# The odd layer's short convolution, one pair of tiles later

## The reference, cut to what matters

```
qkv, z, a, bt = split_cols(h @ w_in, ODD_SPLITS)
qkv = jax.nn.silu(causal_dwconv(qkv, conv_w))     # 4 taps per channel, DN_CONV_K = 4
q, k, v = split_cols(qkv, ...)                    # 1024 channels each, 8 heads of 128
```

## Time and profile before

| what | value |
|---|---|
| median of 3 runs | 2412.43 us |
| the profiled execution | 2412.22 us |
| its span (first to last instruction) | 2410.5 us |
| PE busy | 1926.5 us (80%) |
| DVE busy | 966.3 us (40%) |
| ACT busy | 710.7 us (29%) |
| DMA | mean 252 GB/s |

### The profile page before, as it was taken

How to read it: one execution, slowest core, us unless ns; L and a number is a source line. 1 busy time by engine, 2 the same in 40 slices (tenths; PEclk the granted TensorE clock), 3 DMA queues, 4 the chain that set the end, 5 groups by cost and what they waited for, 6 DMA issues and landing times.

```text
span 2410.5 us, 30262 instructions
## 1 busy us (share of the span) xinstructions
PE 1926.5 (80%) x13238; PEld 1377.4 (57%) x13238; DVE 966.3 (40%) x1730; ACT 710.7 (29%) x1152; POOL 4.1 (0%) x11
## 2 busy tenths in 40 slices
PE   7689998879798999769868888978867765665656
PEld 6589997769678999447644332333255532232323
DVE  6866655666656665354462010101064510100101
ACT  5355444453434444334432000000034410000000
POOL 0000000000000000000000000000000000000000
PEclk9899999799999999989989999999988888888788
DMA  6234454321276445841134999999932379999997
GB/s 246 96 140 162 140 193 181 118 96 71 74 265 229 171 169 199 345 177 74 36 140 188 428 428 427 428 427 428 428 126 105 140 302 428 427 428 427 427 427 325
DMA packets 44787, 606.53 MB, mean 252 GB/s; under 512 B 5104, under 2 KB 5232, under 8 KB 6768
## 3 DMA queue, kind: packets, MB, share of 16 engines
q1 hardware_dynamic: 43488, 597.61, 61.2%
q0 software_dynamic: 880, 4.98, 0.6%
q10 hardware_dynamic: 288, 2.02, 0.2%
HBM read 603.54 MB, written 1.05 MB: 251 GB/s over the span
## 4 chain that ended last, share of the span: by engine, by line
PE 50%; DMA 27%; DVE 14%; ACT 6%; issue 2%; SPq 0%; DVEq 0%; ACTq 0%
PE ps L85 48%; DMA m_last_slot<-moe_down 15%; DMA m_more<-moe_up 9%; DVE m_WL L94 2%; PE ps L88 2%; ACT m_WH L91 1%; ACT m_mix_sc L91 1%; DVE m_od_low L100 1%; DMA m_ring<-ada 1%; DVE m_misc L103 1%; DVE m_wk L94 1%; DVE m_ev L94 1%; ACT m_od_low L91 1%; DVE m_misc L112 1%; ACT L91 1%
## 5 line engine op out<-in xcount | busy, mean ns | idle before, releaser
L85 PE MATMUL ps<-m_ring,m_moe_sc 128*32 128x256 f32 (+1 forms) x2304 | 416.0, 544 | 85.1 <-DMA m_ring<-moe_gate 79.2
L94 DVE TENSOR_TENSOR m_WL<-m_ring,m_WH 128x1024 fp32r<-128x1024 f32 (+1 forms) x277 | 330.4, 1202 | 271.5 <-ACT m_WH L91 270.8
L91 ACT ACTIVATE m_WH<-m_ring 128x1024 fp32r<-128x1024 f32 (+1 forms) x277 | 282.9, 1034 | 124.3 <-PE ps L85 120.9
L85 PEld LDWEIGHTS ps<-m_ring,m_moe_sc 128*32 128x32 f32 (+1 forms) x2304 | 151.7, 143 | 236.2 <-issue 122.2
L85 PE MATMUL ps<-m_more,m_moe_sc 128*32 128x256 f32 (+1 forms) x768 | 208.5, 557 | 82.2 <-DMA m_more<-moe_up 82.2
L85 PE MATMUL ps<-m_nH,m_WH 128*128 128x256 f32 x936 | 238.0, 290 | 15.2 <-ACT m_WH L91 15.2
L85 PE MATMUL ps<-m_nL,m_WH 128*128 128x256 f32 x936 | 237.5, 290 | 9.0 <-DVE m_nL L100 8.8
L94 DVE TENSOR_TENSOR m_nT<-ps,m_nT 128x512 f32<-128x512 f32 (+1 forms) x32 | 17.9, 558 | 558.0 <-PE ps L85 558.0
L91 ACT ACTIVATE m_nT<-ps 128x512 f32<-128x512 f32 (+1 forms) x64 | 31.4, 490 | 622.4 <-PE ps L88 323.9
L85 PE MATMUL ps<-m_last_slot,m_nT 128*32 128x256 f32 (+1 forms) x768 | 184.7, 493 | 30.9 <-DMA m_last_slot<-moe_down 30.9
L85 PE MATMUL ps<-m_more,m_nT 128*32 128x256 f32 (+1 forms) x768 | 187.6, 494 | 18.6 <-ACT m_nT L91 18.6
(11 more groups left out here) (304 smaller groups left out, 3109.7 us busy)
## 6 DMA issues: line engine op xcount, KB each, us to landing
m_ring<-moe_gate SPq DMA_DIRECT2D x64, 2048.0 KB, 19.0
m_ring<-moe_up SPq DMA_DIRECT2D x32, 2048.0 KB, 17.3
m_more<-moe_up SPq DMA_DIRECT2D x32, 2048.0 KB, 21.8
m_more<-moe_down SPq DMA_DIRECT2D x32, 2048.0 KB, 18.0
m_last_slot<-moe_down SPq DMA_DIRECT2D x32, 2048.0 KB, 22.6
m_ring<-ada SPq DMA_DIRECT2D x24, 2048.0 KB, 8.5
m_ring<-ffn_down SPq DMA_DIRECT2D x16, 1408.0 KB, 6.0
m_ring<-ffn_gate SPq DMA_DIRECT2D x10, 2048.0 KB, 8.1
```

What stands on the lines that cost most here:

```text
L85: return Issued() if self.dry else self.e.matmul(out, lhsT, rhs, start=start, stop=stop, skip_group_check=skip)
L91: return Issued() if self.dry else self.e.activation(*a, **k)
L94: return Issued() if self.dry else self.e.tensor_tensor(*a)
```

## The change

`take` on both engines keeps steps 1 and 2 for its own pair and does steps 3 and 4 for the pair before, which it finds in a list `late`. At the end of a call's q, k, v tiles a last call empties the list: before z in `project(H, ..3)`, or, where z isn't in the call, when the job is next resumed. Each call of `project` has a list of its own, so the first pair of each call does no taps and no SiLU.

More of the change, by code:

```diff
@@ L1558, in take @@
                                               ALU.mult).then_inc(*V.mark(("ou", H, w, j), ("out", ("qkv", H, w), j)))
-                            dve.wait_ge(*V.now()).wait_ge(*at(("tap0", H, w, j + n - 1)))
[L1560 to L1566, removed]
+                            taps()
+                            late.append((dst, w, j))
                         yield from dve_dense(4, 8, take)
+                taps()
                 if 3 in what:
```

## The result

The changed kernel took 2393.3 us (median of 5 runs, 2389.39 to 2401.57) against 2412.03 us before (2408.41 to 2413.97): ratio 0.993, 95% interval 0.9908 to 0.9951. The forecast was 2401.2 us with a range from 2397 to 2407: right in direction, too small in size, and the time lies outside the range.

The account below looks back on a forecast made before the run. Before mix(0) it took DVE and ACT handing work to each other as the limit, not PE, at 8.37 us a pair without overlap. Terms A to I sum to -11.0 us: 2412.2 to 2401.2 us, range 2397 to 2407.

Parts of the forecast that it names:

- A: Half 0, pair 1's to pair 2's ou: no taps or SiLU of pair 1 between them, -3.2 us.
- B: Pairs 3 to 6 of half 0: each of four periods loses tap 0's 1.01 us, -4.0 us.
- C: End of q, k, v before z: second set of taps in place of tap 0 delays unit 14's hi, +1.7 us.
- D: PE's clock at z: idle time before unit 14 grows to about 4.0 us, more time lost at 1.2 GHz, +0.9 us.
- E: Fill 2 of mix(0): decay exponentials start 3.5 us earlier, and 0.7 us more for pair 2's ou.
- F: Fills 4 and 5: two sets of taps make the inverse start later relative to ou, all exposed, +2.9 us.
- G: Fill 10, level 5: PE's 3.02 us idle time goes, and 1.8 us lost to the clock, -4.8 us.
- H: Fills 12 and 14: each loses tap 0 from the chain, -2.0 us.
- I: finish behind mix(0): two sets of taps back to back before half 1's last SiLU, +1.7 us.
- R2: More gain: clock stays at 2.4 GHz where idle times shrink, D is nothing; about 2399 us, or 2397; chance 0.12.
- R4: Slower: projection limited by PE, gains vanish, put-off work piles up at each call's end; 2418.5 us; chance 0.04.
- R3: SiLU's table load exposed at three places, 2405.0 us, or 2403.7 with a drain before it; chance 0.06.

Follow-up runs that it names:

- e4: Kernel before with tap 0's ACT instructions left out (weight taken as one), nothing put off; 2403.98 us, ratio 0.9963.
- e5: Changed kernel, but the first pair of each call does its taps and SiLU at once; 2404.82 us, ratio 0.9969 to the kernel before.
- e9: Kernel before, unchanged, run once more for a second profile; 2407.38 us.
- e6: Kernel before with the SiLU alone put off by a pair, taps in place; 2396.01 us, ratio 0.9932.
- e8: Changed kernel with the list emptied behind z's first splits and the SiLU another piece later; 2388.31 us, ratio 0.9904 to the kernel before.

## Why the prediction was too small

By its own terms, against the means of two profiles before and three after:

| term | forecast | measured |
|---|---|---|
| A, pair 1 to 2 | -3.2 | -3.3 |
| B, four periods | -4.0 | -4.6 |
| C and D, end before z and clock | +1.7, +0.9 | +1.4 together |
| E, fill 2 | -4.2 | -4.6 |
| F, fills 4 and 5, to fill 10 | +2.9 | +2.9 |
| G, level 5 | -4.8 | -5.2 |
| H, fills 12 and 14 | -2.0 | -2.3 |
| I, end of `mix(0)` | +1.7 | +1.5 |
| sum (unrounded) | -11.0 | -14.1 |

The mechanism was right at every place, those where it loses included: two sets of taps with `kk` reads between them, PE idle longer before the inverse (3.05 us in two parts before, 6.32 after), a hi for unit 14 6.1 us earlier, `mix(1)` 14.4 us earlier, and the shift kept to the end (15.4 us in the span). Rival R2 had two things right, D at nothing and a full clock in the pairs ahead of z; but inside the levels there was more time at 1.2 GHz than before, not less. Rival R4 would have needed PE as the limit; its clock was full through pairs 3 to 5. R3 is out: tap 0 ends 0.02 us before the load and the exponentials start 0.01 us behind it in fill 2, so a drain has no room on either side, and SiLU starts 0.02 us behind the taps, 0.4 us after the load's end.

Two terms look better in the table than they are. F's +2.9 is the mean of 2.0, 3.3 and 3.4: the inverse starts 2.6 us later behind `ou` (8.2 before, 10.8 after) and not 2.9, and the spread is the clock's, which the term left out. A's is the mean of two profiles at -3.5 and one at -2.9, where PE ran at 1.2 GHz for part of the time; the prediction had PE through by then. That both means fall on the forecast is luck.

The steps that failed are terms of the sum that were mis-sized:

- **The handing over**, in B, C, H and I. I took the price of tap 0 as the time from its start to the taps' start, 1.01 us. A pair saves 1.14 us: 0.94 for tap 0 (e4) and 0.2 because taps that needn't wait follow `ou` more closely. Their first two take 0.80 us in the chain and not 0.89, and nothing stands between `ou` and them. A second set of taps costs 2.6 us and not 2.74. In these four terms together this is some 1.3 us.
- **The clock at z**, term D. PE's idle time grew to 3.72 us, as forecast (4.0). But the stretch behind it has 0.78 over 7.70 us, 3.4 us at 1.2 GHz, as behind 2.23 us before. The 6.8 us that went with the same 3.72 us of idle time ahead of pair 3 were no measure for it; 0.7 of them lay in the idle time itself, as a finer cut of the trace before shows:

```profile
456.24:459.96 3.72, 0.00 (x0) 0.00 (x0) 2.01 (x6) 2.17 (x4) 0.00 (x0) 0.90 0.00 0
459.96:462.40 2.44, 2.44 (x11) 2.44 (x12) 2.44 (x3) 0.90 (x1) 0.00 (x0) 0.50 0.00 0
462.40:465.00 2.60, 2.60 (x14) 2.60 (x13) 1.52 (x4) 0.91 (x2) 0.00 (x0) 0.50 0.74 164
465.00:467.50 2.50, 2.50 (x19) 2.50 (x18) 1.62 (x4) 0.81 (x2) 0.00 (x0) 0.79 0.96 406
```

  D was 0 in these three profiles: 0.9 us. It isn't always. In e5, whose code at z is the same, the 3.74 us of idle time there ended at 487.68, and behind it PE had 5.4 us at 1.2 GHz (7.70 x 0.35 x 2):

```profile
483.94:487.68 3.74, 0.00 (x1) 0.00 (x1) 2.03 (x6) 1.74 (x4) 0.00 (x0) 0.80 0.00 0
487.68:495.38 7.70, 7.70 (x23) 6.13 (x24) 4.56 (x4) 3.59 (x4) 0.00 (x0) 0.65 0.58 200
```

  From pair 6's `ou` to pair 1's of half 1 it took 29.5 us there and 28.6 us in the other three. So D was 0 or 0.9 by the draw, inside the bounds of 0 and 1.7 that the prediction gave.
- **E and G** by 0.4 each. In fill 2 the first profile before gives 4.35 us, close to the bound of 4.3; the rest is e9, where PE ran longer at 1.2 GHz there (0.67 over 7.11 us, 4.7 us, and in the first profile 3.4). G's 3.0 of idle time and 1.8 of clock both went, as forecast; what gave 0.4 more is not shown.

With these terms at their measured sizes the sum is -14.1 us and the forecast 2398.1 us, which still lies inside the range. So the mis-sized terms alone don't put the time outside it. The last 4.8 us to 2393.3 are not in any term: 0.2 come from a base of 2412.2 in place of 2412.03, 0.4 from outside the span, and for some 4.2 no run shows the cause. Against the mean of all eleven runs only 1.7 us of these are left, so most of them are the draw of the first five.

And a fault that isn't in a term: the range. I built it from the mechanism alone and let three runs within 2 us stand for the scatter. Since then single runs of the kernel before lay between 2407.4 and 2415.5 us, of the changed one between 2389.4 and 2401.6. Medians scatter less (2411.95 to 2412.78 in four sets of the kernel before, 2393.3 and 2395.74 in two of the changed one). With a standard deviation of 3.4 us, a median of five runs has an error of some 1.9 us (an estimate), so the range needed about 2 us more on each side for it alone, and still 2393.3 would have lain outside, with 2395.74 inside.

What the prediction didn't look for is what e6 and e8 found: that SiLU and hi stand behind the taps on ACT, and that putting off the SiLU alone is worth as much as the whole change. No run moves the taps without the SiLU.

## What to carry to other kernels

When two engines hand a tile back and forth and each then goes on to the next tile's work in program order, write the period down as a chain with each engine's next independent instruction in it: what gains is to move the waiting instruction behind that next one, and the cheapest such move (here one SiLU on ACT) can be worth as much as the pipeline stage that was built. Count a software pipeline's ends as terms of their own, and ask of each in which fill it falls: the first call without its late part was worth 5.2 us where PE waited for that engine, and a last one with two sets of taps cost 1.4 to 2.9. And take the run-to-run scatter of both kernels into the range, not only the unknowns of the sum.

## What the runs showed of the hardware

- The activation table load started right behind the ACT instruction before it when that stood between the wait for `ou` and the wait for the taps, and only after the wait when nothing did (445.16 in e4): removing an instruction exposed 1.28 us that it had covered, at five places.
- The same idle time of PE, 3.7 us, was followed by 6.1 us at 1.2 GHz ahead of pair 3 in the kernel before, by 5.4 us at z in e5 and by 3.4 us at z in the changed kernel. An idle time of 6.1 us before the inverse was followed by 3.6 us in one run of the changed kernel and by 6.5 and 6.6 us in two others (granted, in the first two: 0.50 over 1.3 us, then 0.90 and 0.78 over 11.7). The cost of a fall of the clock is known to no better than 1.5 us a time from one profile.
- In the pairs ahead of z, idle times of 1.2 us in each 7.2 left the granted clock at 1.00, where it had been 0.81 and 0.78 behind 3.72 us; behind z's wait it was 0.80 with 2.23 us and 1.00 with 1.31 (e4). So shorter waits gave clock back as well. But a fall doesn't need a long wait just ahead of it. In the first profile of the changed kernel the clock fell again at 501 us, with PE busy and no idle time over 1 us since 487.31:

```profile
501.00:503.00 2.00, 2.00 (x13) 2.00 (x13) 0.76 (x5) 1.16 (x2) 0.00 (x0) 0.61 0.00 0
503.00:505.00 2.00, 2.00 (x11) 2.00 (x11) 1.93 (x6) 0.35 (x2) 0.00 (x0) 0.54 0.00 0
```
